# HGRN state stepped over 128 tokens with two reference points in a hybrid decoder step on eight cores

## The chip, the cores and the metric

The kernel runs on all eight cores of one Trainium2 chip. Every core runs the same program on its own part of the batch: one prompt of 2048 tokens and 16 sampled sequences of 8 tokens. Nothing is exchanged between cores. The time is the device time in microseconds (us) of the slowest core, and the result of a kernel is the median of its runs. On each core work TensorE (PE in the profile: matrix products), VectorE (DVE), ScalarE (ACT: activation functions, copies), GpSimd (POOL: elementwise work on SBUF, and it issues the weight loads) and SyncE (SP: it issues the other DMAs).

## What is computed

One decoder layer. From the normalised input come eight projections; two branches, a recurrence (branch A) and a chunked gate (branch B), are merged and added to the input; then follow a convolutional feed-forward part and a gated embedding. The change touches branch A and one line of branch B:

```python
fg = lb + (1.0 - lb) * sigmoid(f_pre)            # forget gate, per head and key
# S_t = diag(f_t) S_{t-1} + k_t v_t^T ,  o_t = S_t^T q_t      with k = 1 - fg, q = silu(q_pre)
b = cumsum(log fg)                               # inside a chunk
o_inter = (q * exp(b)) @ S
scores  = q_t . k_s * exp(b_t - b_s)  for s <= t
S = exp(b_end) * S + (k * exp(b_end - b))^T v
# branch B: v = layernorm(gelu(v_pre)); u * (tril(W_s) v + b) in chunks of 128
```

There are four heads with a 128 x 128 state each. The reference chooses chunks of 64 tokens; any chunk length gives the same sums.

## The kernel before

The program is one list of operations that a planner inside the kernel puts in order. Each operation is written down with its reads and writes (`Prog.op`), and `Prog.schedule` (L234) goes through them with costs of its own (`Emit.act` L510, `Emit.tt` L528, `Emit.ts` L536, `Emit.stt` L545) and decides the order on each engine and the PSUM bank of each result. The engines then execute that fixed order, each strictly in its queue's order, with semaphore waits between them. If one operation changes, the whole order is planned anew.

The work has four stages. In stage 1A the prompt is done in four units of 512 tokens (`unit_1a`, L807, q = 0 to 3), with the 16 sample sequences as a unit of their own between the second and the third. Then come 1B (gates, merge, output projection), 2A (up-projection and convolution) and 2B (down-projection, embedding, final norm). The change lies in 1A alone. Weights of 1B are loaded by GpSimd's queue into the memory that 1A's weights leave, so each load waits for the last use of a weight of 1A; the second of them is w_a (L1129), which four VectorE operations scale when it has landed.

A prompt unit goes like this.

- Heads (loop at L813, four times): TensorE projects f and q (8 products of 128 x 512 each). ScalarE takes tanh of f and then its logarithm; VectorE forms k = 1 - f (`E.ts`, L824), a running sum R of log f that starts anew every 32 tokens (`op_scan`, L832), and subtracts the value at a chunk's middle (L842). GpSimd copies two end values and adds two columns of R into `ge`, the factor from one chunk's reference point to the next. ScalarE takes exp(R) and exp(-R); VectorE multiplies them onto q and k (`qt`, and `kt`, L849). TensorE transposes `kt` (`kh`, copied by VectorE, L854) and multiplies `kt` by `qt`; VectorE masks the result (`sc`).
- The norm of the next unit (`norm_in`, L699) follows in the list: four squares on ScalarE, a product with ones on TensorE, two activations, and eight `E.stt` on VectorE that write the next unit's input.
- Then the projections of i and og, and the state steps (loop at L892): eight steps of 64 tokens. TensorE computes two steps' updates at a time from 64-row halves of `kh` and `vts`. For each step GpSimd computes G = ge * T (T is the state of the step before), ScalarE copies G as bf16 into `sb`, and VectorE adds the update: T = G + update. So T goes through GpSimd and VectorE once for each step.
- Outputs (loop at L912): per head four products of 128 columns (scores) and eight of 64 columns (`sbs` with `qt`) add up in one bank; VectorE gates the result. The third and fourth og projections are written after the first two outputs, because their buffers (`pTG`, two) come free there.
- Branch B: projections of v, with gelu, statistics, two small GpSimd operations and one `E.ts` (L948) that subtracts the mean, multiplies by the reciprocal deviation and writes bf16; projections of u; the mixing products; `E.stt`, and a product on GpSimd that is stored.

In the trace `arena` is all of SBUF and `bank` all of PSUM. The operations have the line of their helper: L583 and L581 products, L591 transposes, L525 activations, L533 `tt`, L542 `ts`, L548 `stt`, L554 copies, L564 the running sum.

## Time and profile before

| | |
|---|---|
| median of 3 runs | 1094.39 us (1092.85 to 1095.41) |
| the profiled execution, device time | 1095.7 us |
| its span on the slowest core (core 3) | 1094.1 us |
| spans of the eight cores | 1088.0 to 1094.1 us |
| busy in the span: PE, DVE, ACT, POOL | 1034.2, 687.0, 557.7, 429.3 us |
| chain of work that ended last | PE 79%, DMA 8%, DVE 4%, issue 3%, ACT 2%, POOL 2% |

The span counts from the first to the last instruction of the core; 1.6 us of the device time lie around it. Products are pipelined, so the busy time of one (353 ns mean) is longer than the distance from one to the next. `[x <-Y]` at the end of a timeline row is the time for which the engine stood idle before it, and who ended that. "128x512 bf16<-128x512 f32 x16 | 15.0, 936" is 16 operations of that form, 15.0 us busy in all, 936 ns the mean. A timeline row with x8 merges eight instructions that follow each other. The stage 1A ends at about 273 us.

### The profile page before, as it was taken

How to read it: one execution, taken by the hardware profiler on the slowest of the kernel's cores; microseconds unless marked ns; L12 is line 12 of the kernel's file. 1: busy time of each engine (PE TensorE's matmuls, PEld its weight loads, DVE VectorE, ACT ScalarE, POOL GpSimd, SP SyncE). 2: the span in 40 equal slices, each digit the busy share in tenths (PEclk: the TensorE clock that was granted, in tenths of full speed). 3: DMA queues.
4: the chain of work that ended last, by engine and by line, in shares of the span. 5: the costliest groups of instructions: out<-in, count | busy, mean ns of one | idle time of the engine just before them, and what ended most of it. 6: DMA issues, size and time to landing. Idle time of an engine off the chain costs nothing.

```text
span 1094.1 us, 19939 instructions; the slowest of 8 cores (1088.0 to 1094.1 us)
## 1 busy us (share of the span) xinstructions
PE 1034.2 (95%) x5658; PEld 493.5 (45%) x5658; DVE 687.0 (63%) x1125; ACT 557.7 (51%) x1068; POOL 429.3 (39%) x578
## 2 busy tenths in 40 slices
PE   4969989898999999999999999999999999999994
PEld 1424454444444445644444444555444444444441
DVE  2668766878445664554888888898998333333333
ACT  3658677484422432222667667888766222222222
POOL 1032344545223833332543444655433333333331
PEclk9989999999999999999999999999999999999997
DMA  8944152469975697946891213950666465364421
GB/s 182 187 128 130 61 170 78 145 119 194 207 252 194 188 283 125 240 157 134 183 180 41 66 42 88 160 112 25 154 189 181 134 166 169 101 173 102 101 78 67
DMA packets 81851, 155.50 MB, mean 142 GB/s; under 512 B 41296, under 2 KB 48208, under 8 KB 78416
## 3 DMA queue, kind: packets, MB, share of 16 engines
q1 hardware_dynamic: 72672, 118.51, 35.7%
q0 software_dynamic: 9072, 35.72, 20.7%
q8 instruction: 48, 0.79, 0.3%
q14 instruction: 59, 0.48, 0.2%
HBM read 129.91 MB, written 51.10 MB: 165 GB/s over the span
## 4 chain that ended last, share of the span: by engine, by line
PE 79%; DMA 8%; DVE 4%; issue 3%; ACT 2%; POOL 2%; POOLq 0%; SPq 0%; DVEq 0%; ACTq 0%
PE bank L583 78%; DMA arena<-w_in 3%; DMA arena<-xpT 2%; ACT arena L525 2%; DVE arena L548 2%; DVE arena L533 1%; DMA arena<-w_a 1%; POOL arena L533 1%; POOL arena L554 1%; DMA o_hs<-arena 1%; PE bank L581 1%; ACT L525 1%; DMA arena<-st_h 1%; DVE arena L542 1%; DVE arena L564 0%
## 5 line engine op out<-in xcount | busy, mean ns | idle before, releaser
L583 PE MATMUL bank<-arena 128*128 128x512 bf16 (+2 forms) x5334 | 1022.4, 353 | 40.9 <-ACT arena L525 17.8
L583 PEld LDWEIGHTS bank<-arena 128*128 128x128 bf16 (+1 forms) x5334 | 476.7, 98 | 571.3 <-issue 72.5
L533 POOL TENSOR_TENSOR arena<-arena 128x512 bf16<-128x512 f32 (+7 forms) x411 | 359.5, 881 | 365.2 <-DVE arena L548 162.5
L548 DVE SCALAR_TENSOR_TENSOR arena<-bank,arena 128x511 f32<-128x511 f32 (+3 forms) x502 | 315.4, 658 | 62.1 <-PE bank L583 22.1
L525 ACT ACTIVATE arena<-arena 128x512 f32<-128x512 f32 (+8 forms) x317 | 212.8, 690 | 261.4 <-DVE arena L533 109.8
L525 ACT ACTIVATE arena<-bank,arena 128x512 f32<-128x512 f32 (+1 forms) x264 | 183.9, 705 | 93.0 <-PE bank L583 90.9
L525 ACT ACTIVATE arena<-bank 128x2 f32<-128x2 f32 (+5 forms) x403 | 140.6, 358 | 160.5 <-PE bank L583 127.4
L533 DVE TENSOR_TENSOR arena<-arena,bank 128x512 f32<-128x512 f32 (+1 forms) x121 | 78.6, 658 | 126.2 <-PE bank L583 113.0
L548 DVE SCALAR_TENSOR_TENSOR arena<-arena 128x512 f32<-128x512 f32 (+5 forms) x113 | 98.3, 890 | 79.7 <-ACT arena L525 63.3
L548 DVE SCALAR_TENSOR_TENSOR arena<-arena,bank 128x512 f32<-128x512 f32 (+2 forms) x108 | 70.3, 655 | 74.7 <-ACT arena L525 45.6
L540 POOL TENSOR_SCALAR arena<-arena 128x1 f32<-128x1 f32 x67 | 18.2, 272 | 153.6 <-ACT arena L525 148.0
L533 DVE TENSOR_TENSOR arena<-arena 128x4 f32<-128x4 f32 (+3 forms) x122 | 44.5, 378 | 10.8 <-ACT arena L525 5.3
L525 ACT ACT_TABLE_LOAD x32 | 41.1, 1283 | 15.9 <-DMA arena<-xpT 6.6
L554 POOL COPY arena<-arena 128x1 f32<-128x1 f32 x28 | 11.7, 417 | 76.8 <-DVE arena L564 75.2
L542 DVE TENSOR_SCALAR arena<-arena 128x512 f32<-128x512 f32 (+2 forms) x36 | 26.1, 730 | 10.6 <-ACT arena L525 6.2
L564 DVE TENSOR_TENSOR_SCAN arena<-arena 128x512 f32<-128x512 f32 x17 | 21.8, 1303 | 14.9 <-ACT arena L525 14.9
L499 POOL DMA_DIRECT2D arena<-w_up x22 | 13.0, 590 | 11.6 <-POOL arena L533 11.0
L581 PEld LDWEIGHTS bank<-arena 128*128 128x128 bf16 x256 | 13.1, 104 | 7.4 <-issue 5.1
L558 DVE BATCH_NORM_STATS2 arena<-arena 128x6 f32<-128x512 f32 x17 | 11.5, 683 | 6.6 <-ACT arena L525 6.5
L554 DVE CAST arena<-arena 128x1024 bf16<-128x1024 f32 (+1 forms) x19 | 13.6, 717 | 3.0 <-DVE arena L533 2.4
L499 POOL DMA_DIRECT2D arena<-ppT x16 | 10.1, 630 | 13.5 <-PE bank L583 10.8
L581 PE MATMUL bank<-arena 128*128 128x64 bf16 (+2 forms) x256 | 14.0, 204 | 1.3 <-ACT arena L525 1.1
(22 smaller groups left out, 69.8 us busy)
## 6 DMA issues: line engine op xcount, KB each, us to landing
arena<-w_up POOLq DMA_DIRECT2D x22, 512.0 KB, 9.7
d_g<-arena SPq DMA_DIRECT2D x20, 512.0 KB, 3.0
arena<-d_g SPq DMA_DIRECT2D x20, 512.0 KB, 8.1
arena<-xpT SPq DMA_DIRECT2D x16, 512.0 KB, 7.7
arena<-w_in POOLq DMA_DIRECT2D x8, 1024.0 KB, 18.0
arena<-xp SPq DMA_DIRECT2D x16, 512.0 KB, 8.4
d_h<-arena SPq DMA_DIRECT2D x16, 512.0 KB, 6.7
arena<-d_h SPq DMA_DIRECT2D x16, 512.0 KB, 4.8
```

The costliest lines, as they stand in the source:

```text
L499: return self.g.op(eng, lambda e: e.dma_start(out=dst, in_=src), reads, writes, dur, dma=nbytes, shift=shift, extra=extra)
L525: return self.g.op("act", lambda e: e.activation(out=_rv(out), in_=_rv(in_), func=func, **kw), reads, writes, dur, tset=TSET.get(func))
L533: return self.g.op(eng, lambda e: e.tensor_tensor(out=_rv(out), in0=_rv(a), in1=_rv(b), op=op), reads, writes, dur)
L540: return self.g.op(eng, lambda e: e.tensor_scalar(out=_rv(out), in0=_rv(a), scalar1=s1, scalar2=None, op0=op0), reads, writes, dur)
L542: return self.g.op(eng, lambda e: e.tensor_scalar(out=_rv(out), in0=_rv(a), scalar1=s1, scalar2=s2, op0=op0, op1=op1), reads, writes, dur)
L548: return self.g.op("dve", lambda e: e.scalar_tensor_tensor(out=_rv(out), in0=_rv(a), scalar=s, in1=_rv(b), op0=op0, op1=op1), reads, write ...
L554: return self.g.op(eng, lambda e: e.tensor_copy(out=_rv(out), in_=_rv(a)), reads, writes, dur)
L558: return self.g.op("dve", lambda e: e.bn_stats(out=out, in_=a), reads, writes, dur)
L564: return self.g.op("dve", lambda e: e.tensor_tensor_scan(out=out, data0=d0, data1=d1, initial=0.0, op0=ALU.mult, op1=ALU.add), reads, writ ...
L581: r = e.matmul(_rv(out), l, rh, start=st, stop=sp, skip_group_check=True)
L583: r = e.matmul(_rv(out), l, rh, start=st, stop=sp)
```

## The change

The state is stepped once for 128 tokens, four times in a unit instead of eight. A block of 128 tokens keeps the two reference points that its two halves of 64 had, at the middle of each half, so that `qt` and `kt` of each half are as before. What connects the two halves and the state is rescaled on GpSimd, for each head:

- `ge` (eight factors a head) is exponentiated by ScalarE per head, 8 columns each, instead of once for the four heads with 32 columns.
- `gab`: the product of a block's two factors, a GpSimd operation of 4 columns.
- `kt` has 1024 columns: the keys of both halves as they are and, in between, the first half's keys times the second half's factor (GpSimd, 256 columns).
- `q2`: the queries times the factor of the first half, or of both (GpSimd, two operations of 256 columns).

The scores of one head are eight products of 64 columns instead of four of 128, and the mask covers the whole lower triangle of 128. They now stand before the transposes. Updates are four products of 128 rows for a block of 128 tokens instead of eight of 64 rows. Outputs use four products of 128 columns with `sbs` instead of eight of 64. G = gab * T on GpSimd, and `sb` is now a copy of T of the step before, not of G.

The factor 1 - f is no longer formed: tanh is taken of -f/2, its logarithm is in a tile of its own, the half of 1 - lb goes into exp(-R) as a bias (`lnh`, its logarithm, formed once at the start), and `kt` is made by `E.stt` as (tanh + 1) * exp(-R). In branch B the normalisation is an `E.stt` whose second operand is the deviation broadcast along the row. `qt` has 3 buffers instead of 5 (its long-lived part is now `q2`, 5 buffers) and `sb` 5 instead of 8. The core of the diff:

```diff
-    pGE = L.pool(32, F32, 2, nsub=4); pDL = L.pool(4, F32, 3, nsub=4)
-    pQT = L.pool(512, BF16, 5); pKT = L.pool(512, BF16, 3); ...
-    pG = L.pool(512, F32, 2); pT = L.pool(512, F32, 3); pSB = L.pool(512, BF16, 8)
+    pGE = L.pool(32, F32, 2, nsub=4); pGB = L.pool(16, F32, 2, nsub=4); pDL = L.pool(4, F32, 3, nsub=4)
+    pQT = L.pool(512, BF16, 3); pQ2 = L.pool(512, BF16, 5, nsub=2); pKT = L.pool(1024, BF16, 3, nsub=2); ...
+    pG = L.pool(512, F32, 2); pT = L.pool(512, F32, 3); pSB = L.pool(512, BF16, 5)
...
-            E.act(tf.ap, p.f(), AF.Tanh, [p], [tf], scale=0.5)
-            k = pK.new()
-            E.ts(k.ap, tf.ap, nhoml(h), homl(h), ALU.mult, ALU.add, [tf, lbt], [k], rate=2.0)
-            E.act(tf.ap, tf.ap, AF.Ln, [tf, lbt], [tf], scale=homl(h), bias=omh(h), psum=False)
+            E.act(tf.ap, p.f(), AF.Tanh, [p], [tf], scale=-0.5)
+            lf = pK.new()
+            E.act(lf.ap, tf.ap, AF.Ln, [tf, lbt], [lf], scale=nhoml(h), bias=omh(h), psum=False)
...
+            E.tt(gh, R3[:, :, 32], R3[:, :, 0], ALU.add, [R], [(ge, h)], eng="pool")
+            E.act(gh, gh, AF.Exp, [(ge, h)], [(ge, h)], psum=False)
+            E.tt(gabh, gh2[:, :, 0], gh2[:, :, 1], ALU.mult, [(ge, h)], [(gab, h)], eng="pool")
...
-            E.act(R[:, 1:513], R[:, 1:513], AF.Exp, [R], [R], scale=-1.0, psum=False)
+            E.act(R[:, 1:513], R[:, 1:513], AF.Exp, [R, lnh], [R], scale=-1.0, bias=lnh[:, h:h + 1], psum=False)
...
-            E.tt(kt.ap, k.ap, R[:, 1:513], ALU.mult, [k, R], [kt])
+            E.stt(ktw, tr_, 1.0, Rv, ALU.add, ALU.mult, [tf, R], [(kt, 0)])
+            E.tt(kt3[:, :, 1, :], kt3[:, :, 0, :], gh2[:, :, 1:2].broadcast_to([P, 4, 64]), ALU.mult,
+                 [(kt, 0), (ge, h)], [(kt, 1)], eng="pool")
+            q2 = pQ2.new()
+            E.tt(v2(q2.ap)[:, :, 0, :], v2(qt.ap)[:, :, 0, :], gh2[:, :, 0:1].broadcast_to([P, 4, 64]), ALU.mult,
+                 [qt, (ge, h)], [(q2, 0)], eng="pool")
+            E.tt(v2(q2.ap)[:, :, 1, :], v2(qt.ap)[:, :, 1, :], gabh.unsqueeze(2).broadcast_to([P, 4, 64]), ALU.mult,
+                 [qt, (gab, h)], [(q2, 1)], eng="pool")
...
+            E.mms([(p.f(i * P + e * 64, i * P + e * 64 + 64), kt[:, i * 256 + e * 64:i * 256 + e * 64 + 128],
+                    qt[:, i * P + e * 64:i * P + e * 64 + 64], True, True)
+                   for e in range(2) for i in range(4)], [kt, qt], [p])
...
-        for c in range(8):
-            i = c // 2
-            if c % 2 == 0:
-                pu = [g.ps(), g.ps()]
-                E.mms([(pu[e].f(h * P, (h + 1) * P), ks[h][e * 64:e * 64 + 64, i * P:(i + 1) * P],
-                        vts[i][e * 64:e * 64 + 64, h * P:(h + 1) * P], True, True)
-                       for h in range(4) for e in range(2)], ks + [vts[i]], pu)
-            p = pu[c % 2]
+        for i in range(4):
+            p = g.ps()
+            E.mms([(p.f(h * P, (h + 1) * P), ks[h][:, i * P:(i + 1) * P], vts[i][:, h * P:(h + 1) * P], True, True)
+                   for h in range(4)], ks + [vts[i]], [p])
...
-                E.tt(h4(G.ap), h4(T_prev[0].ap), ge[:, c * 4:(c + 1) * 4]..., ALU.mult, [T_prev[0], ge], [G], eng="pool")
+                E.tt(h4(G.ap), h4(T_prev[0].ap), gabv[:, i, :]..., ALU.mult, [T_prev[0], gab], [G], eng="pool")
+                E.tt(T.ap, G.ap, p.f(), ALU.add, [G, p], [T])
                 sb = pSB.new()
-                E.act(sb.ap, G.ap, AF.Copy, [G], [sb], psum=False)
-                sbs[c] = sb
-                E.tt(T.ap, G.ap, p.f(), ALU.add, [G, p], [T])
+                E.act(sb.ap, T_prev[0].ap, AF.Copy, [T_prev[0]], [sb], psum=False)
+                sbs[i] = sb
...
-            E.ts(vn.ap, vg.ap, ms[:, 0:1], ms[:, 1:2], ALU.subtract, ALU.mult, [vg, ms], [vn], rate=1.6)
+            E.stt(vn.ap, vg.ap, ms[:, 0:1], ms[:, 1:2].broadcast_to([P, 512]), ALU.subtract, ALU.mult, [vg, ms], [vn])
```

## Rows read from the trace of the kernel before

**Rows 1.** The page's 40 equal slices of the span: busy tenths of TensorE.

```profile
PE   4969989898999999999999999999999999999994
```

**Rows 2.** Windows: busy us of each engine (instructions), clock, DMA share, GB/s.

```profile
55.00:110.00 55.00, 44.35 (x269) 21.22 (x268) 40.25 (x63) 39.05 (x56) 18.61 (x28) 0.91 0.43 127
110.00:165.00 55.00, 50.21 (x407) 27.97 (x406) 38.38 (x64) 40.41 (x66) 21.91 (x30) 0.97 0.37 115
165.00:220.00 55.00, 48.32 (x276) 22.56 (x275) 42.37 (x74) 31.98 (x51) 26.15 (x34) 0.96 0.36 113
220.00:275.00 55.00, 51.69 (x370) 26.44 (x369) 42.67 (x69) 35.45 (x61) 27.22 (x41) 0.98 0.79 157
```

**Rows 3.** Timeline, 75 to 95 us: start, duration, engine, operation, count, idle before.

```profile
74.36 5.84 DVE L548 SCALAR_TENSOR_TENSOR arena<-arena 128x512 bf16<-128x512 f32 x8 [0.59 <-ACT arena L525]
...
80.45 3.57 PE L583 MATMUL bank<-arena 128*128 128x512 bf16 x8 [6.14 <-DVE arena L548]
...
83.81 2.78 PE L581 MATMUL bank<-arena 128*128 128x128 bf16 x44
...
86.57 3.61 PE L583 MATMUL bank<-arena 128*128 128x512 bf16 x16
```

**Rows 4.** Timeline of TensorE alone, later holes and half-clock runs, 108 to 276 us.

```profile
143.30 3.15 PE L583 MATMUL bank<-arena 128*128 128x512 bf16 x8 [0.29 <-DVE arena L548]
...
218.73 3.48 PE L583 MATMUL bank<-arena 128*128 128x512 bf16 x8 [0.21 <-DVE arena L533]
...
261.07 9.35 PE L583 MATMUL bank<-arena 128*128 128x512 bf16 x48 [1.98 <-ACT arena L525]
```

**Rows 5.** Timeline, 200 to 225 us: state steps of the third prompt unit.

```profile
203.40 0.68 DVE L533 TENSOR_TENSOR arena<-arena,bank 128x512 f32<-128x512 f32 x1
...
204.28 1.04 POOL L533 TENSOR_TENSOR arena<-arena 128x512 f32<-128x512 f32 x1 [6.00 <-DVE arena L533]
...
205.48 0.69 DVE L533 TENSOR_TENSOR arena<-arena,bank 128x512 f32<-128x512 f32 x1
...
221.99 2.15 PE L581 MATMUL bank<-arena 128*128 128x128 bf16 x48
```

**Rows 6.** Lines by form, VectorE, first 285 us: count, busy us, mean ns, idle before.

```profile
L533 DVE TENSOR_TENSOR arena<-arena 128x512 bf16<-128x512 f32 x35 | 23.4, 707 | 3.7 <-ACT arena L525 3.3 <-DMA arena<-c_late 0.4
L548 DVE SCALAR_TENSOR_TENSOR arena<-arena 128x512 bf16<-128x512 f32 x32 | 23.3, 785 | 15.5 <-ACT arena L525 15.4
L533 DVE TENSOR_TENSOR arena<-arena,bank 128x512 f32<-128x512 f32 x33 | 22.4, 679 | 6.6 <-POOL arena L533 6.2 <-DVE arena L548 0.2
...
L542 DVE TENSOR_SCALAR arena<-arena 128x512 bf16<-128x512 f32 x16 | 15.0, 936 | 3.8 <-POOL arena L533 3.8
...
L542 DVE TENSOR_SCALAR arena<-arena 128x512 f32<-128x512 f32 x17 | 10.6, 635 | 4.9 <-ACT arena L525 4.5 <-POOL arena L533 0.3
```

**Rows 7.** Lines by form, GpSimd, the whole kernel.

```profile
L533 POOL TENSOR_TENSOR arena<-arena 128x512 bf16<-128x512 f32 x138 | 176.9, 1284 | 217.4 <-ACT arena L525 108.9 <-DVE arena L548 93.3 <-DMA d_ob<-arena 9.0
...
L533 POOL TENSOR_TENSOR arena<-arena 128x512 f32<-128x512 f32 x83 | 98.7, 1195 | 90.9 <-DVE arena L548 34.2 <-DVE arena L533 25.0 <-DVE arena L561 15.0
...
L533 POOL TENSOR_TENSOR arena<-arena 128x128 bf16<-128x128 f32 x30 | 13.8, 458 | 9.2 <-DVE arena L548 6.6 <-ACT arena L525 1.2 <-POOL arena L533 0.2
```

**Rows 8.** Lines by form, ScalarE, first 285 us.

```profile
L525 ACT ACTIVATE arena<-arena 128x512 bf16<-128x512 f32 x31 | 19.5, 630 | 25.9 <-POOL arena L533 25.8
...
L525 ACT ACTIVATE arena<-arena 128x32 f32<-128x32 f32 x3 | 0.7, 220 | 0.1
```

**Rows 9.** Timeline, 176 to 200 us: GpSimd beside VectorE in the third unit's heads.

```profile
193.69 3.69 DVE L533 TENSOR_TENSOR arena<-arena 128x512 bf16<-128x512 f32 x6
...
195.36 2.92 POOL L533 TENSOR_TENSOR arena<-arena 128x512 f32<-128x512 f32 x1 [3.79 <-ACT arena L525]
```

**Rows 10.** Timeline of the weight loads into TensorE, around 127 us: half-row group.

```profile
126.84 1.74 PEld L583 LDWEIGHTS bank<-arena 64*128 64x128 bf16 x16 [0.42 <-issue]
```

**Rows 11.** Timeline, 250 to 280 us: VectorE waits for a weight.

```profile
256.62 0.49 DVE L540 TENSOR_SCALAR arena<-arena 128x1024 bf16<-128x1024 bf16 x1 [1.02 <-DMA arena<-w_a]
```

62 lines of the change are left out of this document (33 added, 29 removed).

## The prediction, written before the changed kernel was run

> **What bounds the kernel now.** I read the 40 slices of the page first, to see in which stage TensorE is not full: from the eleventh slice on (273 us) it shows 9 until the last, so 1B, 2A and 2B are bound by products, and only what comes before can give time [rows 1]. Then the windows over 1A. TensorE is busy for 44.35, 50.21, 48.32 and 51.69 us of four stretches of 55 us, so 25.4 us are idle (10.65, 4.79, 6.68, 3.31), and its granted clock is 0.91 to 0.98 there: for 2 x (1 - clock) x 55 = 9.9, 3.3, 4.4 and 2.2 us it stood at 1.2 GHz instead of 2.4 [rows 2]. VectorE is busy for 163.7 of these 220 us, GpSimd for 93.9 [rows 2]. Then the timelines, for what the holes wait for.
>
> The largest hole is 6.14 us, at 74 to 80.45 us: the second unit's heads wait for VectorE's eight `stt` of the norm (5.84 us). The first unit's outputs (2.78 us) and its third and fourth og projections (3.61 us) run only behind it, from 83.81 us on, because they wait for the last state steps [rows 3]. After the hole eight products take 3.57 us where sixteen at the higher clock take 3.61 [rows 3]; the same is seen behind the second and third units' state steps, 3.15 and 3.48 us for eight, with small holes around them [rows 4]. In the third unit the first T ends at 204.1 and the outputs start at 221.99: 18 us, with the hop from one T to the next 2.08 us where nothing delays it (GpSimd 1.04, VectorE 0.69, the rest hand-over) [rows 5]. So part of the lost time hangs on the state chain, part on the norm of the next unit, part on heads, and in the last unit 1.98 us on an activation [rows 4], just behind VectorE's wait for w_a [rows 11].
>
> **The change part by part.** *State chain.* Before, a unit's outputs needed seven steps after its first T; now the last `sb` is a copy of the third T, so two hops and a copy: 2 x 2.08 + 0.63 [rows 5, 8] = 4.8 us plus hand-overs, say 6, against 18. That is 12 us of latency a unit, but only what TensorE idles for is worth time:
> - First unit: outputs and og (2.78 + 3.61 = 6.4 us) can move into the 6.14 us hole, as the chain then takes 6 us instead of 18; the norm's eight `stt` stay. I take 6; ends 0 and 9.5 (the hole, 1.8 us of half clock behind it, 3.57 for eight products against 1.8, and some of the 4.5 us of smaller holes).
> - Second unit: of its 4.79 us idle and about 1.35 of half clock I take 3; ends 0 and 6.
> - Third: 6.68 idle, which heads, the sample and the state steps share, and 1.7 of half clock; I take 3; ends 0 and 6.
> - Fourth: I take 1; ends 0 and 3.3. Here VectorE's queue stands before w_a [rows 11], and the DMA engines are 0.79 busy [rows 2], so finishing earlier meets a weight that lands no earlier. Weight loads of 1B also stand in GpSimd's queue behind its new operations; each can be late by one of them (0.7 to 2.9 us, below).
>
> *TensorE's own work.* Scores and outputs keep their columns. The sixteen pairs of updates become sixteen groups of full height. Before each half-row group the weight loads stand still for 0.42 us [rows 10]. I take 0.2 us saved for each group, 3 us; ends 0 and 16 x 0.42 = 6.7. The Trainium skill, TensorEngine Tiling (Array Packing), Key Properties, says that independent row tiles run in parallel but that a change of the mode drains the engine; by the parallel part alone this term would be 0, and the 0.42 us speaks for the drain.
>
> *VectorE* loses the `ts` of k (16 x 0.635 = 10.2 us), 16 of 31 additions of T (16 x 0.679 = 10.9) and 16 x (0.936 - 0.785) = 2.4 in branch B, and pays 16 x (0.785 - 0.707) = 1.2 for `kt` by `stt` [rows 6]: 22 us less of 163.7. *ScalarE* loses 16 copies (10.1 us) and gains 12 small exponentials (2.6) [rows 8]; the bias operand of exp(-R) has no row of its own, between 0 and one small activation (0.22) each; I take half, 1.8. *The three start-up operations for `lnh`* lie beside the first weight loads, which TensorE waits for; cost 0, or one small activation if that cover is gone. All this is off the end's path; its worth is in the terms above.
>
> *GpSimd* loses 16 of 31 products G (16 x 1.195 = 19.1 us) and gains 48 operations of 256 columns. Between the 128-wide (0.458) and the 512-wide (1.284) form that is 0.73 each, 35.2 us, and 16 small ones of at most 0.458 [rows 7]: 16 to 23 us more of 220, still not the bound. But one is now on the heads' path: transposes and scores wait for the rescaled keys, which wait for `kt`, in a queue where a `q2` operation may be in front. That is 0.73 + up to 0.73, 1.5 us a head with hand-overs small. Twelve of sixteen heads have projections of the next head or of i and og in front of TensorE; the last head of each unit gates its first update. I charge 4 x 1.5 = 6 us; ends 0 (v projections cover it) and 16 x 1.5 = 24.
>
> *Sum*: 6 + 3 + 3 + 1 + 3 - 6 = 10 us less. The profiled execution took 1095.7 us (span 1094.1 and 1.6 around it), 1.3 above the median of the runs, so the sum gives 1085.7 for it and about 1084.4 for the median. The planner orders everything anew; I know no sign for that, and put it at a hole of the small kind either way, 2 us.
>
> **The rivals.** *A. GpSimd takes the place of the state chain (slower).* In the third unit a G that takes 1.04 us alone took 2.92 us while VectorE ran six products from two SBUF tiles [rows 5, 9]. The new operations stand beside just those (sum, subtraction, `qt`, `kt`). If the three of a unit's last head stretch alike, 3 x 0.73 x 2.8 = 6.1 us lie in front of the first update, 24.5 us in four units; against the 16 us of gains that is 8.5 slower, 1102.9. It decides from the point where TensorE has less than 6 us of projections left when the last `kt` is done. For it: VectorE is the fullest of the three in heads. Against it: VectorE loses 22 us, and the i projections of a unit (32 products, 7.2 us at the pace of the og projections [rows 3]) are written behind its heads. The Trainium skill, SBUF - State Buffer, Who interferes with whom, says that a VectorE operation with two SBUF inputs and a GpSimd operation that reads SBUF exclude each other for their whole length; the 2.92 us agrees. By that rule all 35.2 us added are taken from VectorE or given up to it.
>
> *B. The holes are not the chain's.* The 6.14 us hole ends with the norm, the last with w_a. If the state steps were covered anyway, only TensorE's 3 us remain, and half of the heads' 6 us go against it: 1094.4, no change.
>
> *C. All holes of the state stretches close*: 9.5 + 6 + 6 + 3.3 + 3, with heads covered, gives 28 less; 1066.5. Against it: holes of this kind seldom close all at once, since the norm's 5.84 us stay.
>
> **How the numbers follow.** Forecast 1084.5 (from 1076 to 1091, some gains and costs at half or one and a half): 0.53. A: 0.18. B: 0.16. C: 0.08. The rest, 0.05, is a new order that is better or worse by more, on both sides. The range 1071 to 1099 leaves out most of C and the upper half of A. A measurement of this kernel can tell about 0.2%, 2.2 us, from no change. Faster: the forecast, C and 0.02 each of B and the rest, 0.65. Same: 0.12 of B and 0.01 of the rest, 0.13. Slower: A and 0.02 each of B and the rest, 0.22.
>
> **What would show it.** In the changed profile 15 products G and 15 additions of T instead of 31; a unit's outputs about 6 to 8 us behind its first T; no hole of 6 us in front of the second unit's heads; TensorE's idle in the four windows near 16 us instead of 25, and fewer stretches at 1.2 GHz; VectorE busy about 20 us less before 275 us, GpSimd about 20 more. The 48 operations near 0.73 us: right; near 2 us: A. If TensorE waits for GpSimd in heads, term by term the last was too low. If the end of 1A moves by 10 us and the end of the kernel does not, a weight or a load behind it is late, which none of my terms has. The stages behind 1A should keep their length (from 273 us to the end of the span, 821 us); if they change, the sum is wrong in a place that I did not look at.

## The result, and the profile after

The changed kernel is slower: 1.0101 times the time before, 95% interval 1.0074 to 1.0128. The five runs that are compared took 1102.3 to 1110.7 us, against a median of 1094.5 us before; three more, up to 1129 us, are left out, since cores of one die show a lower granted clock in them, and two of the five (1109.1 and 1110.7) have cores with such a clock too (0.95 to 0.97), without which the kernel is 0.7 to 0.8% slower. The profiled execution took 1103.4 us, forecast 1085.7 for it; its spans are 1093.4 to 1101.2 us on the eight cores.

Four marks in the traces divide the work: the issue of the last unit's state store (the state work of 1A ends), the first stored row block of `d_h` (the first product of 1B), the first stored block of `d_g` (the first of 2A), and the end. Means over the eight cores, in us:

| kernel | state stored | to first d_h | to first d_g | to the end | end |
|---|---|---|---|---|---|
| before | 269.1 | 52.3 | 214.4 | 555.6 | 1091.4 |
| after | 267.5 | 56.8 | 217.8 | 555.4 | 1097.5 |
| difference | -1.6 | +4.5 | +3.4 | -0.2 | +6.1 |

So the stage that was changed is 1.6 us shorter where I expected 10, and 1B, where no line was changed, is 7.9 us longer. Windows over 1A and the first of 1B, in the columns of [rows 2] (core 2, the longest):

```profile
55.00:110.00 55.00, 43.98 (x256) 21.22 (x260) 37.17 (x56) 39.76 (x58) 22.71 (x34) 0.94 0.40 129
110.00:165.00 55.00, 50.82 (x383) 28.75 (x388) 38.63 (x66) 33.15 (x56) 23.31 (x38) 1.00 0.38 119
165.00:220.00 55.00, 45.71 (x271) 23.51 (x273) 40.62 (x62) 36.55 (x58) 29.79 (x47) 0.88 0.31 112
220.00:275.00 55.00, 51.86 (x342) 27.00 (x348) 40.95 (x64) 36.41 (x63) 35.87 (x53) 1.00 0.82 169
275.00:330.00 55.00, 49.30 (x216) 21.88 (x219) 20.41 (x30) 15.62 (x26) 13.92 (x12) 0.94 0.77 202
```

In the four windows of 1A TensorE is idle for 11.02, 4.18, 9.29 and 3.14 us, 27.6 in all; it was 25.4. VectorE has 157.4 us of work instead of 163.7 (the forecast took 22 off), ScalarE 145.9 instead of 146.9 (forecast: 5.7 off), GpSimd 111.7 instead of 93.9 (forecast: 16 to 23 on). These are windows of one core each, without the first 55 us; in the means over the eight cores, up to 275 us, VectorE has 9.9 us less, ScalarE 3.2 less and GpSimd 24.9 more. The fifth window lies in 1B, and 5.7 us of it are idle. Seen from the page's slices of TensorE (core 4), against [rows 1], such a hole is the 7 in the eleventh place:

```profile
PE   4979898799799999999999999999999999999994
```

The first hole of 1A, to be read beside [rows 3]: timeline, 72 to 85 us.

```profile
72.78 1.84 PE L581 MATMUL bank<-arena 128*128 128x128 bf16 x28
...
73.85 5.38 DVE L548 SCALAR_TENSOR_TENSOR arena<-arena 128x512 bf16<-128x512 f32 x8
...
79.97 4.42 PE L583 MATMUL bank<-arena 128*128 128x512 bf16 x10 [5.35 <-DVE arena L548]
```

The outputs, at 83.81 us before, are now done ahead of the hole, and the hole is still 5.35 us, to the end of the same eight `stt`. In the third unit TensorE now waits for the rescaled keys, and the price of the new operations and of `stt` shows by form (VectorE and GpSimd, first 285 us, columns as in [rows 6]):

```profile
208.33 0.39 PE L583 MATMUL bank<-arena 128*128 128x64 bf16 x8 [3.13 <-POOL arena L533]
```

```profile
L548 DVE SCALAR_TENSOR_TENSOR arena<-arena 128x512 bf16<-128x512 f32 x64 | 57.4, 933 | 20.0 <-ACT arena L525 17.0 <-POOL arena L533 2.9
...
L533 POOL TENSOR_TENSOR arena<-arena 128x256 bf16<-128x256 bf16 x48 | 38.2, 823 | 11.8 <-DVE arena L533 9.4 <-DVE arena L548 2.2
```

The 48 operations take 0.823 us (forecast 0.73), and the `stt` form 0.933 where [rows 6] has 0.785. Next, 1B: timeline, 284 to 325 us.

```profile
287.54 2.49 POOL L533 TENSOR_TENSOR arena<-arena 128x512 bf16<-128x512 f32 x2 [13.12 <-DMA o_hp<-arena]
...
288.89 2.31 ACT L525 ACTIVATE arena<-bank 128x512 f32<-128x512 f32 x4 [8.12 <-POOL arena L533]
...
320.16 3.19 PE L583 MATMUL bank<-arena 128*128 128x512 bf16 x7 [5.54 <-POOL arena L533]
```

GpSimd stands for 13 us until the store of the last state (`o_hp`) has landed, ScalarE stands behind GpSimd, and 32 us later TensorE is out of work. All eight cores have such holes, 3.7 to 6.9 us together between 270 and 335 us (0 to 1.3 before). The cause is in the layout of SBUF: the final state `fs` takes a buffer of `pG` in 1A. Before, the memory of that buffer became `qTB` in 1B (tiles that ScalarE writes later); with the new pools of 1A it lies 6304 bytes further on and becomes a part of `qM`, the tile into which GpSimd merges the branches first. Later in 1B there is one more hole, at the sample unit (TensorE, 454 to 470 us; then the instruction fetches of TensorE's queue, 459 to 460.5 us: packets, MB, share):

```profile
454.83 3.57 PE L583 MATMUL bank<-arena 128*128 128x128 bf16 x61
461.51 8.65 PE L583 MATMUL bank<-arena 128*128 128x128 bf16 x65 [3.11 <-issue]
```

```profile
q8 instruction: 1, 0.02, 4.0%
```

No operation is waited for there ("issue"). All eight cores have it, 0.65 to 3.1 us, and on all eight a 16 KB packet of instructions for TensorE lands 1.3 to 1.6 us before the products resume.

### The profile page after: what moved, and what is told of

Same layout as the page of the kernel before. It is cut to its first block, busy times and chain, and to the rows that moved or that the text cites. A ratio compares the mean times of both kernels' runs of the same rounds, so it can differ in the third digit from the quotient of the medians.

```text
span 1100.4 us, 19720 instructions; the slowest of 8 cores (1093.4 to 1101.2 us)
## 1 busy us (share of the span) xinstructions
PE 1027.9 (93%) x5491; PEld 496.4 (45%) x5594; DVE 676.1 (61%) x1094; ACT 551.7 (50%) x1064; POOL 455.6 (41%) x630
## 4 chain that ended last, share of the span: by engine, by line
PE 78%; issue 5%; DVE 5%; POOL 4%; DMA 4%; ACT 3%; POOLq 0%; DVEq 0%; SPq 0%; ACTq 0%
PE bank L583 77%; POOL arena L533 3%; ACT arena L525 3%; DVE arena L548 2%; DMA o_hp<-arena 2%; DMA arena<-xpT 2%; DVE arena L533 1%; POOL arena L554 1%; ACT L525 1%; DVE arena L564 0%; PE bank L581 0%; PE bank L591 0%; DVE arena L554 0%; DVE arena L558 0%; POOL arena L540 0%
## 5 line engine op out<-in xcount | busy, mean ns | idle before, releaser
L583 PE MATMUL bank<-arena 128*128 128x512 bf16 (+1 forms) x5231 | 1016.8, 353 | 56.3 <-ACT arena L525 18.8
L583 PEld LDWEIGHTS bank<-arena 128*128 128x128 bf16 x5334 | 482.8, 99 | 582.1 <-issue 81.3
L533 POOL TENSOR_TENSOR arena<-arena 128x512 bf16<-128x512 f32 (+9 forms) x459 | 387.5, 853 | 349.1 <-DVE arena L548 158.0
L525 ACT ACTIVATE arena<-arena 128x512 f32<-128x512 f32 (+7 forms) x314 | 206.1, 675 | 249.7 <-DVE arena L533 116.0
L525 ACT ACTIVATE arena<-bank 128x2 f32<-128x2 f32 (+4 forms) x403 | 139.9, 356 | 185.0 <-PE bank L583 133.0
L548 DVE SCALAR_TENSOR_TENSOR arena<-arena 128x512 bf16<-128x512 f32 (+5 forms) x145 | 129.2, 911 | 103.4 <-ACT arena L525 85.3
L533 DVE TENSOR_TENSOR arena<-arena,bank 128x512 f32<-128x512 f32 (+1 forms) x105 | 68.0, 654 | 127.2 <-PE bank L583 112.5
L533 DVE TENSOR_TENSOR arena<-arena 128x4 f32<-128x4 f32 (+3 forms) x106 | 35.4, 338 | 16.1 <-ACT arena L525 8.0
L533 DVE TENSOR_TENSOR arena<-bank,arena 128x512 bf16<-128x512 f32 x17 | 11.6, 680 | 7.4 <-PE bank L583 7.4
L581 PEld LDWEIGHTS bank<-arena 128*128 128x128 bf16 x192 | 11.0, 97 | 6.1 <-issue 2.7
L581 PE MATMUL bank<-arena 128*128 128x128 bf16 (+1 forms) x192 | 12.4, 202 | 0.9 <-DVE arena L533 0.8
```

What stands on the lines that cost most here:

```text
L525: return self.g.op("act", lambda e: e.activation(out=_rv(out), in_=_rv(in_), func=func, **kw), reads, writes, dur, tset=TSET.get(func))
L533: return self.g.op(eng, lambda e: e.tensor_tensor(out=_rv(out), in0=_rv(a), in1=_rv(b), op=op), reads, writes, dur)
L548: return self.g.op("dve", lambda e: e.scalar_tensor_tensor(out=_rv(out), in0=_rv(a), scalar=s, in1=_rv(b), op0=op0, op1=op1), reads, write ...
L581: r = e.matmul(_rv(out), l, rh, start=st, stop=sp, skip_group_check=True)
L583: r = e.matmul(_rv(out), l, rh, start=st, stop=sp)
```

## The experiments

Theory after the result: the chain is worth what I said; GpSimd's new operations take more than they were charged in 1A; and the layout and the place of an instruction block lengthen 1B. Rivals: the state chain is worth little (B of the prediction); the loss in 1A lies in the small parts (1 - f folded into the exponential, LayerNorm by `stt`) or in the order that the planner makes of it all. "Mended layout" below means a buffer of its own for `fs`; "g0" is the changed kernel with that and four buffers `pOB`.

**Layout: e1 and f1.** The changed kernel, where only `fs` moves (e1); the kernel before with the mended layout and four `pOB` (f1).

```diff
-    ... pOB = L.pool(512, BF16, 2)
+    ... pOB = L.pool(512, BF16, 2); pFS = L.pool(512, F32, 1)
-            fs = pG.new()
+            fs = pFS.new()
```

> The changed kernel with the final state's buffer in 2 KB of its own behind all other tiles of stage 1A, instead of in a buffer of pG; the order of TensorE's instructions in stage 1A is unchanged. Theory (the layout): in the first unit of 1B the merge on GpSimd waits 8 to 13 us for the store of the final state, because its tile now lies over that buffer, and TensorE stands 3 to 6 us behind it. Then GpSimd's wait for that store goes, the 4 to 6 us hole of TensorE between 290 and 322 us goes, the first store of d_h comes 3 to 5 us earlier (324.3 to about 320, mean of the cores), and the kernel ends 3 to 5 us earlier, at 1098 to 1100 us. Rival (the DMA queues): all transfers there are late since the engines of the DMA are full, so GpSimd or ScalarE waits for another transfer instead; the hole stays over 3 us and the end moves by less than 1 us.

> The kernel before with the final state's buffer in a place of its own and four instead of two buffers for the gate products (ob): the same mending of the layout without the change. Theory (the layout costs only where the change moved it): before, TensorE had no hole of over 1.3 us in the first unit of 1B, so nothing is there to gain; the time stays within 2 us of the kernel before. Rival (the layout was a bound of its own): the first store of d_h comes 3 us earlier and the kernel ends at 1090 to 1092 us, and then the 3 us that the changed kernel with this place is ahead by are the layout's and not the change's.

e1: 0.9992 [0.9961, 1.0022], first `d_h` at 316.6 instead of 324.3, end 1088.4 instead of 1097.5. The window that had the hole (e1, core 5):

```profile
275.00:330.00 55.00, 54.96 (x256) 24.76 (x255) 26.32 (x36) 18.15 (x30) 15.38 (x16) 1.00 0.93 245
```

TensorE has no idle time left there. f1: 0.9987 [0.9977, 0.9998], end 1090.3 against 1091.4. Where `fs` lay well its place was worth about 1 us; the change of the pools made it cost 9.

**Instruction block: e3.** 64 products at the very start, beside the first loads, so that every block of TensorE's instructions ends at another place.

```diff
+    pz = g.ps()
+    E.mms([(pz.f(0, P), onesb.ap, onesb.ap, True, True) for _ in range(64)], [onesb], [pz])
     xns = {0: norm_in(0)}
```

> The changed kernel with 64 more matmuls of 128 columns on TensorE before the first input has landed; every engine's order is otherwise the same. They cost nothing there, for TensorE waits until 17 us anyway. Theory (code loading): the hole of 0.7 to 3.1 us in the sample unit of 1B (at 454 to 461 us, ended by nothing that the trace shows, with an instruction packet landing 1.3 us before its end) is TensorE waiting for its next block of instructions; then it moves to another matmul, 64 matmuls earlier or to no place at all, and if it goes the kernel is 2 to 4 us faster. Rival (a wait for data): the hole stays in front of the same matmul of the sample unit, and the time is that of the changed kernel within 1 us.

1.0036 [1.002, 1.0052]. The place that had the hole, core 5:

```profile
439.70 26.86 PE L583 MATMUL bank<-arena 128*128 128x512 bf16 x266
466.74 13.54 PE L583 MATMUL bank<-arena 128*128 128x512 bf16 x62 [0.18 <-issue]
```

The hole is gone on all cores, with every engine's order otherwise the same, and from first `d_h` to first `d_g` it is 216.1 us instead of 217.8 (before 214.4). But state stored and first `d_h` come later by 0.5 and 1.7 us, and the end is the same, 1097.3. By the ratios e3 is ahead of the changed kernel; its profiled execution is the longest of the seven compared (1097.3 to 1103.4 us). So the cause of the hole is shown, and the size of a gain is open. The hole is also gone in e1 and g0, where no product was added but the order in 1B is another. The other 1.7 of the 3.4 us that this stretch grew have no name yet.

**The chain alone: e4 and f2.** The kernel before with four steps of 128 tokens and nothing else (e4), and with the mended layout and four `pOB` (f2). Both leave out the rescaling between a block's halves.

```diff
-        for c in range(8):
-            i = c // 2
-            ... (two half-row updates)
+        for i in range(4):
+            c = 2 * i
+            p = g.ps()
+            E.mms([(p.f(h * P, (h + 1) * P), ks[h][:, i * P:(i + 1) * P], vts[i][:, h * P:(h + 1) * P], True, True)
+                   for h in range(4)], ks + [vts[i]], [p])
...
-                sbs[c] = sb
+                sbs[i] = sb
```

> The kernel before with the state stepped four times a unit instead of eight, the sixteen update products merged to full rows and the state's products at 128 columns, without any rescaling of keys or queries (so the factors of the halves are left out). It is the part of the change from which the forecast took its gain, without the part from which it took its cost. By the forecast's sum TensorE gains 13 us of holes and 3 us of products: about 1078 us. Rival (the holes of 1A end with the next unit's norm and heads, not with the state): the 6.1 us hole at 80 us keeps at least 5 us, the other holes lose 1 to 2 us together, and the gain is 3 to 6 us: 1088 to 1091 us.

> The four-step state without rescaling (the factors of the halves are left out), as before, and with the final state's buffer in a place of its own and four ob buffers. With neither, TensorE left stage 1A 11.7 us earlier and then stood 12.4 to 15.5 us for ScalarE and GpSimd, which waited 19 and 27 us for the stores of the final state and of ob. Theory (small stores behind the weights swallow the gain): those waits go, the hole at 282 to 290 us falls under 3 us, and the kernel ends 8 to 12 us earlier than the kernel before, at 1082 to 1087 us. Rival (the weights of 1B set the start of 1B): TensorE then waits for a weight of 1B, the hole stays over 8 us, and the time stays at 1092 us or more.

e4: 1.0048 [1.0019, 1.0078], slower although its 1A is 11.7 us shorter (257.4). Timeline, 284 to 292 us (core 2), and what the queues moved from 215 to 300 us (count, KB each, us from issue to landing):

```profile
287.00 2.48 POOL L533 TENSOR_TENSOR arena<-arena 128x512 bf16<-128x512 f32 x2 [26.92 <-DMA d_ob<-arena]
...
287.77 1.28 ACT L525 ACT_TABLE_LOAD   x1 [19.34 <-DMA o_hp<-arena]
...
289.81 2.72 PE L583 MATMUL bank<-arena 128*128 128x512 bf16 x6 [15.53 <-ACT arena L525]
```

```profile
arena<-w_o POOLq DMA_DIRECT2D x2, 1024.0 KB, 20.9
...
o_hp<-arena SPq DMA_DIRECT2D x1, 256.0 KB, 28.6
```

TensorE idles for 13.95 us there in the mean of the cores. The store of the last state takes 28.6 us from issue to landing (13.2 before, on the same core); it moves beside the weight loads of 1B and beside other loads of SyncE's own queue, and which of them holds it up was not told apart. The buffers that this store and those of `d_ob` hold (`fs`, `pOB`) stop ScalarE and GpSimd. f2 gives those buffers room: 0.9841 [0.9822, 0.986], end of 1A 254.6, idle from there to the first `d_h` 0.7 us, end of the kernel 1075.1, 16.3 us before that of the kernel before. Windows of f2 (core 1):

```profile
55.00:110.00 55.00, 47.13 (x256) 22.29 (x255) 34.10 (x55) 37.25 (x53) 16.08 (x24) 0.94 0.43 131
110.00:165.00 55.00, 52.63 (x419) 30.65 (x417) 40.80 (x74) 38.11 (x64) 16.78 (x26) 1.00 0.43 129
165.00:220.00 55.00, 51.48 (x305) 25.25 (x304) 43.41 (x73) 40.50 (x62) 25.15 (x33) 1.00 0.41 121
220.00:275.00 55.00, 53.10 (x312) 26.33 (x310) 37.85 (x64) 33.39 (x54) 25.34 (x39) 1.00 0.99 183
```

Idle are 7.87, 2.37, 3.52 and 1.90 us, 15.7 in all, and by the clock column 6.6 us at 1.2 GHz instead of the 19.8 of [rows 2]. Rival B falls: the chain is worth 15 us (16.3 less the 1.1 of f1).

**GpSimd's operations: g1, e2, g0, f3.** g1 is f2 with 48 products of the same size on GpSimd that nobody reads; nothing waits for a result of theirs, though `kt`, `qt` and R can't be overwritten before they have run. e2 is the changed kernel with the keys' product on VectorE. f3 is g0 with the two products of the queries put behind other work.

```diff
+            for src, e in ((kt, 0), (qt, 0), (qt, 1)):        # g1
+                z = pZ.new()
+                E.tt(z..., v2(src.ap)[:, :, e, :], R3[:, 0:4, 1:2].broadcast_to([P, 4, 64]), ALU.mult, [src, R], [z], eng="pool")
```

```diff
-                 [(kt, 0), (ge, h)], [(kt, 1)], eng="pool")   # e2
+                 [(kt, 0), (ge, h)], [(kt, 1)])
```

```diff
             q2 = pQ2.new()                                   # f3
+            g.prio_shift = 100
             ... (the two products of q2)
+            g.prio_shift = 0
```

> The four-step state without rescaling and with the layout mended (1078.6 us; the factors of the halves are left out), and with three products of 256 columns on GpSimd per head whose results nobody reads. They load GpSimd's queue as the change does (48 products of about 0.82 us, 39 us) but stand in nobody's chain. Theory (the chain: keys, scores and transposes wait in series for GpSimd): the queue alone costs 0 to 4 us, 1078 to 1083 us, and the rest of the 12 us between this and the mended changed kernel is the waiting for the keys. Rival (occupancy: GpSimd's other products, of the state and of the gates, come late behind them): 8 us or more, 1087 us or above.

> The changed kernel with the rescaling of the keys (one 256-column product per head) on VectorE instead of GpSimd; the two products of the queries stay on GpSimd. Theory (GpSimd's queue): in unit 2 the heads' score products wait for the keys behind up to ten GpSimd operations (TensorE idle 3.1, 1.8, 1.3 and 1.5 us between 205 and 216 us); on VectorE each costs about 0.3 us, the four idles fall to under 1 us each, GpSimd is busy 12.7 us less in 1A, the end of 1A comes 5 to 7 us earlier and the kernel ends at 1096 to 1099 us. Rival (the heads are bound by VectorE or by ScalarE's tables): the idle time moves to waits for VectorE, the sum of TensorE's idle time in 1A stays within 2 us of 26, and the time stays within 2 us of the changed kernel.

> The changed kernel with the final state's buffer in a place of its own and four ob buffers, nothing else. It is the base for the kernel with the later query products (1091.0 us) and shows what the ob buffers bring beside the place alone (1093.3 us). Theory (the query products in front of the keys cost): 1092 to 1094 us, 2 to 3 us more than with the later query products, the difference lying in the holes at 205 to 216 us. Rival (the 2 us came from the ob buffers or from another plan): 1090 to 1091.5 us.

> The changed kernel with the layout mended (own place for the final state, four ob buffers) and with the two query products of each head behind the key product in the planner's priority, so that GpSimd takes a ready key product first. Theory (GpSimd's queue holds up the keys): the holes of TensorE between 205 and 216 us (3.1, 1.8, 1.3 and 1.5 us, the first ended by GpSimd) lose 3 us or more together, the sum of TensorE's idle time in 1A falls from 26 to 20 to 23 us, and the kernel ends at 1087 to 1090 us. Rival (a query product is begun before the key product is ready, so its place in the order doesn't matter, or the next engine is late): the idle time stays within 2 us of 26, and the time at 1092 to 1094 us.

g1: 0.9918 [0.9878, 0.9958]; 1A ends at 263.7, 9.1 us behind f2, with nothing waiting for the new results. TensorE's idle in the four windows (core 2) is back at 25.6 us:

```profile
55.00:110.00 55.00, 45.71 (x242) 21.83 (x246) 34.82 (x55) 38.33 (x55) 17.98 (x27) 0.94 0.40 125
110.00:165.00 55.00, 49.50 (x397) 29.12 (x401) 41.44 (x71) 35.30 (x59) 27.76 (x40) 1.00 0.40 129
165.00:220.00 55.00, 47.86 (x276) 23.27 (x280) 45.83 (x73) 41.84 (x62) 33.34 (x44) 0.97 0.33 115
220.00:275.00 55.00, 51.33 (x302) 25.71 (x306) 36.92 (x59) 34.74 (x55) 32.97 (x47) 1.00 0.94 163
```

VectorE's forms from 20 to 270 us, f2 first, then g1:

```profile
L564 DVE TENSOR_TENSOR_SCAN arena<-arena 128x512 f32<-128x512 f32 x17 | 23.2, 1373 | 7.2 <-ACT arena L525 7.2
L533 DVE TENSOR_TENSOR arena<-arena 128x512 bf16<-128x512 f32 x35 | 23.0, 691 | 6.8 <-ACT arena L525 5.0 <-DMA arena<-c_late 1.7
```

```profile
L533 DVE TENSOR_TENSOR arena<-arena 128x512 bf16<-128x512 f32 x35 | 28.3, 839 | 6.3 <-ACT arena L525 4.7 <-DMA arena<-c_late 1.5
L564 DVE TENSOR_TENSOR_SCAN arena<-arena 128x512 f32<-128x512 f32 x17 | 25.0, 1481 | 3.1 <-ACT arena L525 3.1
```

The same operations on VectorE stretch from 691 to 839 ns and from 1373 to 1481, 7.0 us in these two forms alone. The order was planned anew too, but not from the start: apart from the 48, VectorE, ScalarE and GpSimd run the same operations, by tile and form, in the same order in both kernels for 214, 201 and 77 operations, up to 195, 204 and 195 us of f2. There g1 is 5.3, 5.8 and 6.5 us behind (means of the cores), and over its 214 operations VectorE works 6.8 us longer (139.1 to 145.8), ScalarE and GpSimd's other operations no longer than before. So 5 to 6 of the 9.1 us come without a new order, beside a stretch of VectorE of that size; the rest, where the order differs, is not told apart. And g1, g0 and all the kernels below that carry these operations end 1A 8 to 23 us behind f2, none near it.

g0, where the results are needed: 0.995 [0.9934, 0.9966], 1A ends at 265.5, only 1.8 us behind g1. f3: 0.9954 [0.9938, 0.997], 262.5; the same ratio as g0, so the queries' products in front of the keys' cost little that the ratio shows. e2: 1.0072 [1.0037, 1.0106], 1A ends at 271.4, 3.9 us later than in the changed kernel, though one product on VectorE takes 0.643 us against GpSimd's 0.823: I had expected 0.3.

```profile
L533 DVE TENSOR_TENSOR arena<-arena 128x256 bf16<-128x256 bf16 x16 | 10.1, 643 | 0.3
```

Moving the work to the fuller engine did not pay, though a difference of this size can also be order (below).

**The hole of the norm: f4 and g4.** f4: e1 with the input of the next unit released one unit earlier. g4: f3 with f and q of the first two heads projected slice by slice, so that they can start with the first of the eight `stt`.

```diff
-    X1_GATE = prev[-3]                                       # f4
+    X1_GATE = prev[-4]
```

```diff
-            if q == 0 and h == 0:                            # g4, and alike for q's projection
+            if h < 2:
                 for dk in range(8):
```

> The changed kernel with the final state's buffer in a place of its own, and the load of unit 1's input released one weight earlier (by the third of the last four weights of 1A from the end counted one further on, about 8 us earlier). Theory (the hole of 5.35 us at 80 us ends with the next unit's norm, whose eight products on VectorE wait for that input, and not with the state): the hole falls under 2 us, and the kernel gains 3 to 4 us on the one with the place alone (1093.3 us): 1089 to 1091 us. Rival (the hole is VectorE's queue, whenever the input comes): it stays over 4.5 us, and the time stays within 1 us of 1093.3 or is longer, since two weights come later.

> The changed kernel with the layout mended and the later query products (1091.0 us), and with the products of the first two heads of every unit given to TensorE in eight steps, each waiting for its own eighth of the normed input instead of for all of it. Theory (the 5.35 us hole at 80 us is the wait for the eight products of the norm on VectorE): TensorE starts 4 to 5 us earlier there and fills most of the hole, which falls under 2.5 us; the kernel ends 2 to 4 us earlier, at 1087 to 1089 us. Rival (the heads after it are bound by ScalarE and VectorE anyway): the hole splits into small ones, the idle time in 1A stays within 1 us of 23.6, and the time at 1090 to 1092 us.

f4: 1.0084 [1.0055, 1.0112], 1A 8 us longer (core 1):

```profile
82.08 5.39 DVE L548 SCALAR_TENSOR_TENSOR arena<-arena 128x512 bf16<-128x512 f32 x8 [4.04 <-ACT arena L525]
...
87.61 2.72 PE L583 MATMUL bank<-arena 128*128 128x512 bf16 x6 [7.53 <-DVE arena L548]
```

The norm came later, not earlier, and the hole grew to 7.53 us. The edit did not do what it was meant to: the first quarter of the input lands earlier (50.2 us on core 1, 57.9 on core 5 of e1), the last does not (63.9, there 62.6). But the norm's `stt` begin 18 us behind that landing here and 11 us behind it in the changed kernel (62.9 to 73.85), so something else than the input holds them, and my theory fell. g4: 0.9932 [0.9911, 0.9953], 1A ends at 264.6 (core 6):

```profile
78.81 10.62 PE L583 MATMUL bank<-arena 128*128 128x512 bf16 x48 [0.18 <-DVE arena L548]
...
99.48 0.59 PE L583 MATMUL bank<-arena 128*128 128x128 bf16 x4 [4.21 <-DVE arena L548]
```

The hole at 79 us is closed to 0.18, and 4.21 us open twenty microseconds later, with the same releaser line (that of the helper of every `stt`; which one it is, the row does not say). g4 has the lowest ratio of all kernels that compute the layer in full, 0.7% below before, though f3 and g0 lie inside or near its interval.

**The small parts, and order by itself: g3, i2, h2, h1, h3, i1, k1.** g3 is the kernel before with the fold and LayerNorm by `stt`, as in the diff of the change; i2 with the fold alone; h2 with LayerNorm by `stt` alone, given the planner's old duration so that the order stays. h1 is g0 without the two. h3 is the kernel before, its instructions unchanged, with two planner durations set to those measured in [rows 6] (936 and 635 ns). i1 is g0 with g4's slices, the three factors of a block in one tile, one 512-column product for `q2`, and LayerNorm by `ts`. k1 is g0 with one tanh buffer more and one log buffer less.

```diff
+            g.ops[-1].dur = (512 / 1.6 + 200) / 0.96         # h2, behind the stt
```

```diff
+            g.ops[-1].dur = 936.0                            # h3, behind the ts of LayerNorm
+            g.ops[-1].dur = 635.0                            # h3, behind the ts of k
```

```diff
+            E.tt(v2(q2.ap), v2(qt.ap), g3[:, :, 0:2].unsqueeze(3).broadcast_to([P, 4, 2, 64]), ALU.mult,   # i1
+                 [qt, (ge, h)], [q2], eng="pool")
```

```diff
-    pTF = L.pool(512, F32, 3); ... pK = L.pool(512, F32, 3)  # k1
+    pTF = L.pool(512, F32, 4); ... pK = L.pool(512, F32, 2)
```

> The kernel before with two parts of the change alone: 1 - f folded into the exponential and the LayerNorm by one two-operand product on VectorE, without the four-step state. Theory (these parts lie under other work): VectorE is busy 5 to 15 us less in 1A, no hole of TensorE moves by over 1 us, and the time stays within 2 us of the kernel before. Rival (VectorE is the late one in the heads): TensorE's idle time in 1A falls by 3 us or more and the kernel gains as much, 1088 to 1091 us; or, if another plan brings the stores of 1A and the weights of 1B together, it loses 3 us or more.

> The kernel before with 1 - f folded into the exponential alone. The fold and the LayerNorm together made it 0.7% slower (end of 1A 9.8 us later), the LayerNorm alone in the old order 3.8 us of that. Theory (the fold takes 10 us from VectorE and lengthens no chain, so the other 6 us were the order): the end of 1A lies within 3 us of the kernel before, ratio 0.997 to 1.003. Rival (the fold itself costs, by its form on VectorE or ScalarE): the end of 1A comes 5 us or more later, ratio 1.004 to 1.007.

> The kernel before with the LayerNorm by the two-operand product on VectorE and everything in the order of the kernel before (the planner is told the old duration). Theory (order, not duration, made the two small parts slow): the sixteen operations take 0.75 to 0.95 us each as the old form did, and the time is that of the kernel before within 1.5 us. Rival (the new form holds up VectorE or GpSimd): VectorE's or GpSimd's busy time in 1A rises by 4 us or more and the kernel is 2 to 4 us slower.

> The changed kernel with the layout mended (own place, four ob buffers; 1092.8 us, 0.995 of the kernel before) and with 1 - f and the LayerNorm as before: the new state with its rescaling alone. Theory (the two small parts cost VectorE time or latency in the heads, as they cost the kernel before 0.7%): 4 to 8 us less, ratio 0.988 to 0.991, TensorE's idle time in 1A 2 us or more below 24.9. Rival (what the small parts cost the kernel before was its new order alone): within 2 us of the mended kernel, ratio 0.993 to 0.997, or longer.

> The kernel before with the same instructions in another order: the planner is told 0.936 us for the LayerNorm's and 0.635 us for the keys' VectorE operation, as the trace has them, instead of 0.54 and 0.48. No work is added or taken away. Theory (a new order alone moves 1A by as much as a whole part of the change was priced at): the issue of the final state's store moves by 4 us or more from 269.1 us, to either side, and the time by 3 us or more. Rival (the order is worth 2 us, as the forecast had it): both stay within 2 us.

> The changed kernel with the layout mended, the first two heads' products in eight steps, the LayerNorm in its old form, and the two query products of a head merged to one of 512 columns on GpSimd (its factors stand beside each other). Theory (GpSimd's 39 us in 1A cost through its contention with VectorE, 8 us for 41 us of products): 32 products of 256 columns become 16 of some 1.25 us, GpSimd is 6 us less busy, VectorE's LayerNorm 2 to 4 us less; 2 to 3 us on top of the kernel with eight steps (0.993): a ratio of 0.990 to 0.992. Rival (the new order decides): 0.993 to 0.999.

> The changed kernel with the layout mended (own place, four ob buffers; 0.995 of the kernel before) and one buffer moved from the logarithms (pK, three to two) to the tanh results (pTF, three to four). With the fold the tanh result of a head is read until its key product instead of until the logarithm, so with three buffers the fourth head's tanh waits for the first head's key product: in the kernel with the fold alone the fourth tanh came at 47.0 us instead of 37.6, behind another table load. Theory (the life of that buffer is what the fold costs): the fourth head's scan comes at 48 to 50 us instead of 53.0, the end of 1A 2 us or more before 265.5, ratio 0.990 to 0.993. Rival (in the changed kernel GpSimd sets the heads, so the early tanh brings nothing, or the new order takes it): the end of 1A within 2 us of 265.5 or later, ratio 0.994 or more.

| kernel | ratio [95%] | 1A ends, us | end, us |
|---|---|---|---|
| before | 1 | 269.1 | 1091.4 |
| g3, fold and LayerNorm | 1.0072 [1.0049, 1.0095] | 278.9 | 1101.5 |
| i2, fold | 1.009 [1.0075, 1.0105] | 276.0 | 1104.1 |
| h2, LayerNorm, order kept | 1.0027 [0.9992, 1.0062] | 272.9 | 1095.8 |
| h3, another order | 0.9973 [0.9949, 0.9997] | 268.7 | 1088.9 |
| g0 | 0.995 [0.9934, 0.9966] | 265.5 | 1087.1 |
| h1, g0 without the small parts | 0.9988 [0.9968, 1.0008] | 267.1 | 1089.8 |
| k1, g0 with other buffers | 1.0055 [1.0034, 1.0076] | 273.2 | 1096.6 |
| i1, g0 with merged factors | 1.0038 [1.0024, 1.0052] | 277.9 | 1096.7 |

LayerNorm by `stt` takes VectorE longer by itself. In h2 the form holds 16 more operations (core 5, 20 to 270 us):

```profile
L548 DVE SCALAR_TENSOR_TENSOR arena<-arena 128x512 bf16<-128x512 f32 x44 | 39.9, 940 | 4.4 <-POOL arena L533 3.8 <-ACT arena L525 0.4
```

The 16 by themselves, in the order of the 16 `ts` before, take 1.18 us each on every core, against 0.936 for `ts`: 4.0 us more, and 1A ends 3.8 later. The interval of the ratio just takes in 1.

The fold takes 7.0 us of busy time off VectorE in i2 (688.7 to 681.7 us over the kernel, means of the cores), and the kernel is 0.9% slower. By the code, a tanh buffer now lives until the keys are formed, so the fourth head's tanh waits for one and falls behind a table load (i2, core 3; the same tanh is at 37.6 us before):

```profile
45.72 1.28 ACT L525 ACT_TABLE_LOAD   x1
47.01 1.57 ACT L525 ACTIVATE arena<-bank 128x512 f32<-128x512 f32 x3
```

The running sum of the fourth head starts at 52.0 us (before 47.9). k1 tests that: with a fourth tanh buffer it starts at 47.7, as the theory says (53.0 in g0), and yet 1A ends 7.7 us later than in g0. k1 also has one log buffer less, and what that costs was not told apart. But in h1, without the fold, the same sum starts at 53.3, no earlier than in g0; so inside the full change the buffer's longer life is not what holds it, and that theory fell as well. h1 is no faster than g0, so there the small parts cost nothing that shows.

What is left is the order, and it is argued more than shown. f3, g4, g0, h1, k1 and i1 do nearly the same work, and their 1A ends at 262.5, 264.6, 265.5, 267.1, 273.2 and 277.9 us. i1 has the least on GpSimd (416 us of work over the kernel against 422 to 430, means of the cores) and is the last. The 15 us between them (12.5 at the first `d_h`, 13 at the end) come near what the chain is worth. But k1 differs in its buffers and i1 and h1 in their operations too. The one kernel in which nothing but the order changes, h3, moved the end of 1A by 0.4 us, where I had expected 4 or more, and the time by 0.3%. How much of what g3 and i2 lost is order, and how much the parts, stays open.

## Why the prediction was wrong

The end of the kernel, in means over the cores, moved by +6.1 us where -10 was forecast. The experiments make a bridge. Its ends are means over the cores of one profiled execution each. The groups e, f, g and h to k ran on different chips, and there the same mean of the kernel before, over all its runs that are compared, is 1090.7, 1090.9, 1093.6 and 1092.7 to 1093.1 us; so a step from one group to another is uncertain by some 3 us. By the ratios the step from f2 to g1 is 0.77%, 8.4 us.

| step | forecast | measured, end | of it in 1A |
|---|---|---|---|
| before to f2: chain, full-height updates (with f1's -1.1) | -16 | -16.3 | -14.5 |
| f2 to g1: 48 products on GpSimd, unread | 0 | +10.0 | +9.1 |
| g1 to g0: that they are waited for, small parts, order | +6 | +2.0 | +1.8 |
| g0 to the changed kernel: layout, instruction block | 0 | +10.4 | +2.0 |

- *State chain and TensorE's own work.* Right in sum, 16 forecast, 15 to 16 measured. The distribution was off: idle fell by 2.8, 2.4, 3.2 and 1.4 us in the four windows (one core each, and f2's last window lies partly in 1B) where I had 6, 3, 3 and 1. In the means over the cores, from 30 us to the first `d_h`, TensorE has 9.1 us less idle time, loses 3.2 less to the lower clock (7.0 to 3.8, one less the granted clock times the stretch), and is busy 4.6 less beside that, where I had 3 for its own work. I put the outputs into the hole of 6.14 us [rows 3]; they went ahead of it, and the hole stayed because the norm ends it. The 3 us from [rows 10] were not measured apart. The row is one of thirteen such runs on that core, of which seven stand 0.42 us, the others 0.10 to 1.18. From the 512-column product in front of a group to the one behind it, where none waits, the half-row group takes 0.64 us (median of 22) and one of full height 0.44 to 0.66 in f2 (8 groups): 0.2 us each is the most that these rows allow.
- *The heads' GpSimd.* The step that failed in 1A. I charged the new operations as latency in front of a unit's first update, 4 x 1.5, after saying that 35 us of new work are "still not the bound". The latency is at most the 1.8 us of g1 to g0. What they cost is that they are there: 8 to 10 us in g1, where no one waits for them, 5 to 6 of it at a place up to which the order is the same and VectorE's same operations took 6.8 us longer. An engine cost time without being full.
- *VectorE.* 9.9 us less up to 275 us in the means over the cores (6.3 in the four windows), not 22. In the changed kernel the 16 `stt` of LayerNorm take 0.984 us each, 0.8 us more in all than `ts` did instead of 2.4 less (in h2 4.0 more); `kt` by `stt` takes 0.986 us where I had 0.785, 3.2 us in all; and the 32 `stt` of the norm, which were not changed, take 0.879 instead of 0.785, 3.0 us. That is 9.4 of the 12 missing, and the rest has no name. The new `stt` were priced by the row of the norm's, which stand elsewhere. The start-up operations for `lnh` are two in the diff, not three; nothing hangs on it.
- *Nothing behind 1A changes.* The step that failed by most: 10.4 us at the end of the kernel, 8.4 of them in 1B. The prediction named the sign ("the sum is wrong in a place that I did not look at") and the DMA side ("a weight or a load behind it is late"), but gave it no price. It was a store, and a buffer whose memory another stage uses. The diff shows the pool sizes that moved it, and e1 gives back 9.1 us by 2 KB.
- *Order, 2 us either way.* Perhaps too small: like work ended 1A within 15 us, but not by order alone. h3, with the same instructions in another order, gave 0.3%, some 3 us.
- *Rival A* gave 1102.9, and the profiled run took 1103.4; but that is chance, for its way is not what happened. The new operations took 0.823 us, not 0.73 x 2.8, 1A became no longer, and the loss lies in 1B. Its cause, GpSimd beside VectorE, does fit the larger part of what the chain's gain lost in 1A. *B* is refuted by f2, and *C* by the hole of the norm, which no experiment removed without another one opening.

## What to carry to other kernels

Work that is put on an engine with time to spare is charged by what it takes from the engine it shares inputs and queue order with; a test with the same operations unread prices that, as far as the two kernels keep the same order. When tiles of a stage change size, look up what each long-lived buffer, and each one that a store still reads, becomes in the next stage. Where a planner orders everything anew, a few variants with equal work show how much of a difference is order, before a part is credited or blamed; a variant in which the order alone changes says more than several that differ in buffers too.

## What the runs showed of the hardware

VectorE's operations stretch beside GpSimd when two inputs come from SBUF. In the changed kernel, all cores, first 285 us, those overlapped by GpSimd for less than a tenth of their time against those for more than nine tenths: `stt` f32 to bf16 without `kt` 0.743 us (192 operations) against 1.247 (48); `kt` 0.692 (7) against 1.080 (87); the running sum 1.220 (48) against 1.618 (41). With one input from PSUM the `stt` stay at 0.685 and 0.679, and the statistics at 0.685 in both. One form with a single SBUF input stretches too: `ts`, 0.541 against 1.024 us in g1 and 0.540 against 1.184 before. The Trainium skill, SBUF — State Buffer, Who interferes with whom, names the pair (two SBUF inputs against a GpSimd operation that reads SBUF) and an exclusive lock. The pair agrees with these rows, which show factors of 1.3 to 1.7 for it; whether one of the two stands still for the other's whole length, they do not tell. For `ts`, which the page counts among the operations that can take both ports, they show 1.9 to 2.2.

TensorE can run out of instructions: it stood for 0.65 to 3.1 us around the arrival of a 16 KB block, in a stretch of 128-column products (61 in 3.57 us) with the DMA engines near full; with the blocks shifted (e3) it did not, nor with another order in 1B (e1, g0). And a store of 256 KB, issued while loads of 0.5 to 1 MB were moving, landed after 28.6 us in e4, 13.2 in the kernel before.
